# Hybrid encoder layer: ScalarE copies PV's results at the end of their own quarter, and makes V in the second quarter

## The chip, the cores and the metric

One NeuronCore of a Trainium2 chip runs the whole layer in one launch. The metric is device time in microseconds (us) from launch to end, the median of several executions. A profile of one further execution gives the span from the first to the last instruction and what each engine did in it.

## The reference, cut to what matters

```python
# per layer: half FFN, mixer (convolution group + attention), half FFN, final norm
h = h + 0.5 * g1 * _swiglu(_modulate(h, sh1, s1), ffn1_wg, ffn1_wu, ffn1_wd)
z = _modulate(h, shm, smx) @ w_in                 # -> u | cq | ckv | kr
a = u[..., :C_CONV] * sigmoid(u[..., C_CONV:])
a = depthwise_conv(a, conv_w, width 31) + conv_b  # 512 channels
a = silu(_layernorm(a, g_conv_ln, b_conv_ln))
q, k, v = up-projections of cq and ckv, q and k RMS-normed by head, rotary on 32 of 96
def one_block(qblk):
    s = einsum('bqhd,bkhd->bhqk', qblk, k) * scale
    p = softmax(s, axis=-1)
    return einsum('bhqk,bkhd->bqhd', p, v)
h = h + gm * (concatenate([a, att], axis=-1) @ w_out)
h = h + 0.5 * g2 * _swiglu(_modulate(h, sh2, s2), ffn2_wg, ffn2_wu, ffn2_wd)
```

Sequence 1024, model width 1024, 8 heads with 96-wide q and k and 64-wide v.

## The kernel before

**Stages.** The two feed-forward halves take most of the time. Between them stands the mixer; its attention part runs from about 884 us to 1176 us of the span, and the change lies there alone. Every engine has an order of its own, written out by hand, and the engines meet through semaphores.

**Turns and quarters.** `run_units` gives each engine four turns `i` of two heads each. Turn 0 and turn 3 (the last) are written out, and turns 1 and 2 are a loop with a register. A turn has four quarters `m`: quarter `m` handles head `m // 2` of the turn and the half `m % 2` of the 1024 queries. So quarters 0 and 2 are called even, and quarters 1 and 3 odd. A quarter has four steps `p`. Over them:

- PE turns the next head's q and k in even quarters (`pe_turn_head`, L1710, one unit in each step), makes the products for the next quarter's maxima (`pe_max`, L1594), this quarter's scores (`pe_scores`, L1635, six matmuls), and PV of the quarter before (`pe_pv`, L1657, four matmuls) into bank 6. In step 3 it also turns the row of maxima (`pe_max_row`, L1616), between the two halves of that step's PV.
- ScalarE (ACT) casts each turned head unit (`act_head_unit`, L1721), writes the row of maxima into the augmented queries (`act_max`, L1623), takes the exponentials (`act_exp`, L1644), copies PV's finished bank to `grow` (`act_pv_copy`, L1666), spreads V to `vs` (`act_v`, L1688), and makes the products of convolution taps for channel chunks 2 and 3 (`act_prod`, L1806): 2, 1, 2 and 1 in the steps of an even quarter, 0, 1, 2 and 1 in those of an odd one.
- VectorE (DVE) reduces the maxima (`dve_max`, L1602), makes the low part of head units (`dve_head_unit`, L1728, even quarters) or a convolution tap of chunks 0 and 1 (`dve_tap`, L1826, one in each step of an odd quarter), three parts of the reciprocal of PV's denominators in steps 0 to 2 (`dve_pv_recip`, L1673), and in step 3 the scaling into `att` (`dve_pv_scale`, L1681). All of it is for the PV result of the quarter before.
- GpSimd (POOL) adds the products to `cv` (`pool_conv`, L1815 and L1816, two instructions for each product) and, at the start of odd quarters, makes the slots of a coming head (`pool_slots`, L1760, L1762, L1766).

**What ties them.** The waits that the change touches:

```python
def act_pv_copy(e, i, m):
    e.wait_ge(pv_mm, i * 4 + m)                # the PV of quarter m is finished
    if not (isinstance(i, int) and i == 0 and m == 1):
        e.wait_ge(pv_out, i * 4 + (m - 1))     # VectorE has scaled the result before it
```

`pe_pv` may begin a quarter's PV only when the copy of the result before it is made (`pv_copied`) and the exponentials of that quarter are all there. `pe_turn_head` number n waits until VectorE has made the low part of head unit n - 1 (`qk_lo`), which waits for the cast on ScalarE. `act_prod` number n waits until POOL has added product n - 2 (`conv_add`), and `pool_conv` waits for its product (`prod_ok`). `pe_max` waits for the reduction before it (`s_max`), `act_v` for the last PV that reads the old V (`pv_mm`), and the first PV with a new V for `v_ok`.

Before the change ScalarE copies the result of quarter `m - 1` in step 0 of quarter `m`, so behind the product of step 3, and makes V in step 3 of an odd quarter, between `act_max` and the last exponential.

Of the kernel before, what the change touches and what calls it, by code (L numbers as in the profile page):

```python
# [39 lines left out]
def build(nc, A, out):  # L40
# [5 lines left out]
    NH = S // HALF  # L46
# [31 lines left out]
    with ExitStack() as ctx:  # L78
# [1492 lines left out]
        TURNS = NHD // 2  # L1571
        AUG = QK + 1

        def at(i, m):

            return (i + m // NU, m % NU)
# [42 lines left out]
        def act_max(e, i, m):  # L1619
            i, m = at(i, m)  # L1620
            hp, h = divmod(m, NH)
            e.wait_ge(m_row, i * 4 + (m + 1))
            e.activation(qkT[QK:AUG, hp, 0, HI, h * HALF:(h + 1) * HALF], ps[0:1, MISC], ACT.Copy).then_inc(m_ok, 1)  # L1623
# [15 lines left out]
        def act_exp(e, i, m, p):  # L1639
            e.wait_ge(s_mm, i * 16 + (m * 4 + p + 1))  # L1640
            if p == 0 and not (isinstance(i, int) and i == 0 and m < 2):
                e.wait_ge(pv_mm, i * 4 + (m - 1))
            b = 2 + 2 * (p % 2)
            e.activation(EX[m % 2][:, 2 * p:2 * p + 2], ps[:, b:b + 2], ACT.Exp).then_inc(s_exp, 1)  # L1644
# [16 lines left out]
        def act_pv_copy(e, i, m):  # L1661

            e.wait_ge(pv_mm, i * 4 + m)
            if not (isinstance(i, int) and i == 0 and m == 1):
                e.wait_ge(pv_out, i * 4 + (m - 1))
            e.activation(grow[:, 0:HALF], ps[:, 6], ACT.Copy).then_inc(pv_copied, 1)  # L1666
# [16 lines left out]
        def act_v(e, i, hp, first=False):  # L1683

            hd = i * 2 + hp
            if not first:
                e.wait_ge(pv_mm, hd * 2 - 2)
            e.activation(vs[:, hp, :, 0:VH], vn[:, :, bass.ds(hd, 1), :].rearrange("p t a d -> p t (a d)"), ACT.Copy)\  # L1688
                .then_inc(v_ok, 1)
# [27 lines left out]
        def act_head_unit(e, i, hp, n, first=False):  # L1717
            u, bank = head_unit(n, first)
            hp_, m, tok = head_place(hp, u)
            e.wait_ge(qk_turned, i * 8 + (hp * 4 + n + 1))  # L1720
            e.activation(qkT[0:QK, hp_, m, HI, tok], ps[0:QK, bank], ACT.Copy, scale=gains[0:QK, m:m + 1])\  # L1721
                .then_inc(qk_hi, 1)
# [74 lines left out]
        def products(m, p0, p1):  # L1797

            start = m // NH * TT + m % NH * sum(PRODUCTS[0])
            return range(start + sum(PRODUCTS[m % NH][:p0]), start + sum(PRODUCTS[m % NH][:p1]))  # L1800

        def act_prod(e, i, n, first):
            c, k = 2 + n % 2, 1 + n // 2
            if not (first and n < 2):
                e.wait_ge(conv_add, i * (2 * TT) + (n - 1))
            e.activation(prod[:, n % 2], ac[:, c, bass.ds(i * TT + k, S)], ACT.Copy,  # L1806
                         scale=cw[:, c, bass.ds(i * TT + k, 1)]).then_inc(prod_ok, 1)
# [60 lines left out]
        def act_ln_square(e, c):  # L1868
            e.wait_ge(ln_mean, 2 * CC)
            e.activation(squares[c], cv[:, c], ACT.Square).then_inc(ln_act, 1)  # L1870
# [29 lines left out]
        def act_ln_swish(e):  # L1900
            for c in range(CC):
                e.wait_ge(ln_dve, 3 + c)
                e.activation(cv[:, c], cv[:, c], ACT.Silu, bias=vect[:, V_LB + c:V_LB + c + 1],
                             scale=vect[:, V_LG + c:V_LG + c + 1]).then_inc(ln_act, 1)
# [9 lines left out]
        def act_wo_hi(e, c):  # L1914
            e.wait_ge(wo_scaled, c + 1)
            if c == 0:
                e.wait_ge(slot_k, NHD + 1)
            if c == 5:
                e.wait_ge(v_ok, NHD)
            if c == 7:  # L1920
                e.wait_ge(pv_mm, 2 * NHD)
            e.activation(wo[:, c, HI], wor[:, c % 2], ACT.Copy).then_inc(wo_hi, 1)
# [5 lines left out]
        def run_units(e, unit):  # L1928

            for m in range(NU):  # L1930
                unit(0, m, True, False)
            with e.Fori(1, TURNS - 1) as i:
                for m in range(NU):
                    unit(i, m, False, False)
            for m in range(NU):
                unit(TURNS - 1, m, False, True)

        def next_head(i, m):

            return (i, 1) if m // NH == 0 else (i + 1, 0)  # L1940
# [178 lines left out]
        def _(e):  # L2119
# [146 lines left out]

            def unit(i, m, first, last):
                for p in range(THALF):
                    if p == 0 and not (first and m < 2):
                        act_pv_copy(e, *at(i, m - 1))  # L2270
                    if m % NH == 0 and not (last and m // NH == 1):
                        act_head_unit(e, *next_head(i, m), p)
                    if p == 3 and not (last and m == NU - 1):
                        act_max(e, i, m + 1)
                    if last:
                        for c in WO_HI_AT.get((m, p), ())[:1]:
                            act_wo_hi(e, c)
                    if last and m == 2 and p < 2:
                        act_ln_square(e, 2 * p)
                        act_ln_square(e, 2 * p + 1)  # L2280
                    if p == 3 and m % NH == 1 and not (last and m // NH == 1):
                        act_v(e, *next_head(i, m), first=first and m == 1)
                    act_exp(e, i, m, p)
                    if last:
                        for c in WO_HI_AT.get((m, p), ())[1:]:
                            act_wo_hi(e, c)
                    if not last and not (first and m == 0 and p == 0):
                        for n in products(m, p, p + 1):
                            act_prod(e, i, n, first)

            run_units(e, unit)
            act_pv_copy(e, TURNS, -1)
            act_ln_swish(e)
            act_wo_hi(e, KC - 2)
            act_pv_copy(e, TURNS, 0)
# [496 lines left out]
```

## Time and profile before

| what | value |
|---|---|
| median of 3 runs | 1919.88 us (1916.6 to 1920.43) |
| the profiled execution: its own time | 1922.11 us |
| its span, first to last instruction | 1919.9 us |
| mean granted TensorE clock | 0.987 |
| PE busy over the span | 1840.6 us (96%) |
| DVE, ACT, POOL busy over the span | 1392.3, 796.0, 803.7 us |
| stretch 1010 to 1027 us (an odd quarter): PE, DVE, ACT, POOL busy | 15.59, 16.18, 10.62, 16.73 of 17.00 us |
| stretch 1027 to 1044 us (an even quarter): PE, DVE, ACT, POOL busy | 16.45, 14.32, 13.70, 16.29 of 17.00 us |

The shares over the whole span hide that the attention stretch has limits of its own: there PE, DVE and POOL are all busy most of the time, so the rows below are those of single instructions in it. In a timeline row the first number is the start in us from the span's start, the second the duration in us, then engine, line, operation, what it writes and reads, and in brackets the idle time of the engine just before it with what ended it. Durations overlap a little on one engine, because instructions are pipelined.

### The profile page before, as it was taken

How to read it: one execution, taken by the hardware profiler on the slowest of the kernel's cores; microseconds unless marked ns; L12 is line 12 of the kernel's file. 1: busy time of each engine (PE TensorE's matmuls, PEld its weight loads, DVE VectorE, ACT ScalarE, POOL GpSimd, SP SyncE). 2: the span in 40 equal slices, each digit the busy share in tenths (PEclk: the TensorE clock that was granted, in tenths of full speed). 3: DMA queues.
4: the chain of work that ended last, by engine and by line, in shares of the span. 5: the costliest groups of instructions: out<-in, count | busy, mean ns of one | idle time of the engine just before them, and what ended most of it. 6: DMA issues, size and time to landing. Idle time of an engine off the chain costs nothing.

```text
span 1919.9 us, 22681 instructions
## 1 busy us (share of the span) xinstructions
PE 1840.6 (96%) x8043; PEld 1471.2 (77%) x8043; DVE 1392.3 (73%) x1774; ACT 796.0 (41%) x1248; POOL 803.7 (42%) x605
## 2 busy tenths in 40 slices
PE   4999999999999999997999999999999999999997
PEld 3788888878888878985665566877888888888886
DVE  5678888876777785776888877358656555577778
ACT  4542232223344554246676643154332323334453
POOL 1076655666200010019999941014566556520000
PEclk9999999999999999997999999999999999999999
DMA  9045666545653442000000023112333323476333
GB/s 351 12 143 184 222 210 206 198 154 199 251 209 94 124 171 69 4 1 0 1 1 0 0 68 152 66 55 85 107 110 110 107 85 110 170 249 228 96 108 125
DMA packets 132795, 232.11 MB, mean 121 GB/s; under 512 B 8780, under 2 KB 66227, under 8 KB 132434
## 3 DMA queue, kind: packets, MB, share of 16 engines
q1 hardware_dynamic: 132500, 230.73, 35.5%
q8 instruction: 62, 1.02, 0.2%
q14 instruction: 43, 0.35, 0.1%
q10 hardware_dynamic: 190, 0.01, 0.0%
HBM read 177.75 MB, written 52.95 MB: 120 GB/s over the span
## 4 chain that ended last, share of the span: by engine, by line
PE 43%; DVE 6%; POOL 2%; issue 2%; ACT 2%; DMA 0%; DVEq 0%; ACTq 0%; POOLq 0%
PE ps L502 20%; PE ps L854 9%; PE ps L2752 4%; PE ps L1657 3%; PE ps L376 2%; PE ps L1635 2%; DVE cv L1826 1%; PE ps L1594 1%; DVE grow L1673 1%; DVE att L1681 1%; POOL rqk L1751 0%; DVE negmax L1602 0%; ACT prod L1806 0%; PE ps L1710 0%; DVE H L2598 0%
## 5 line engine op out<-in xcount | busy, mean ns | idle before, releaser
L502 PE MATMUL ps<-T,ring 128*128 128x512 f32 x1920 | 441.8, 389 | 0.0
L502 PEld LDWEIGHTS ps<-T,ring 128*128 128x128 f32 x1920 | 360.3, 188 | 75.0 <-DVE ring L479 0.2
L502 PE MATMUL ps<-B,ring 128*128 128x512 f32 x1440 | 338.1, 391 | 5.7 <-DVE SG L561 4.4
L502 PEld LDWEIGHTS ps<-B,ring 128*128 128x128 f32 x1440 | 269.4, 188 | 65.1 <-issue 9.5
L954 POOL TENSOR_SCALAR stat<-stat 128x1 f32<-128x1 f32 x32 | 10.7, 333 | 550.8 <-ACT XS L879 260.0
L568 POOL TENSOR_TENSOR HID<-HID,SG 128x512 f32<-128x512 f32 x80 | 122.2, 1527 | 262.4 <-DVE HID L553 151.5
L854 PE MATMUL ps<-PW 128*128 128x512 f32 x924 | 217.3, 389 | 0.0
L854 PE MATMUL ps<-PT 128*128 128x512 f32 x900 | 212.0, 390 | 0.0
L854 PEld LDWEIGHTS ps<-PW 128*128 128x128 f32 x924 | 173.3, 188 | 36.0
L479 DVE TENSOR_TENSOR ring<-sums,ring 128x512 fp32r<-128x512 f32 x160 | 162.9, 1027 | 52.0 <-ACT ring L473 52.0
L854 PEld LDWEIGHTS ps<-PT 128*128 128x128 f32 x900 | 168.5, 188 | 34.8
L473 ACT ACTIVATE ring<-sums 128x512 fp32r<-128x512 f32 x160 | 97.0, 627 | 158.8 <-PE ps L502 139.8
L522 ACT ACTIVATE SG<-SG 128x512 f32<-128x512 f32 x80 | 50.6, 633 | 245.7 <-DVE SG L553 98.5
L1657 PE MATMUL ps<-E,vs 128*128 128x512 f32 x256 | 125.7, 607 | 10.4 <-ACT grow L1666 10.4
L1602 DVE TENSOR_REDUCE negmax<-ps 128x1 f32<-128x1024 f32 x64 | 77.3, 1211 | 37.5 <-PE ps L1594 37.4
L479 DVE TENSOR_TENSOR ring<-rawu,ring 128x512 fp32r<-128x512 f32 x60 | 66.6, 1120 | 51.9 <-ACT ring L473 51.9
L1635 PE MATMUL ps<-qkT 97*128 97x512 f32 x384 | 103.5, 406 | 0.0
L701 ACT ACTIVATE PW<-adat 128x512 fp32r<-128x512 f32 x77 | 48.6, 631 | 123.9 <-PE ps L854 91.7
L1815 POOL TENSOR_TENSOR cv<-cv,prod 128x512 f32<-128x512 f32 x60 | 88.7, 1478 | 8.8 <-ACT prod L1806 8.6
L701 ACT ACTIVATE PT<-adat 128x512 fp32r<-128x512 f32 x75 | 47.4, 631 | 107.2 <-PE ps L854 92.1
L2752 PE MATMUL ps<-wo,mixT 128*128 128x512 f32 x384 | 88.0, 390 | 2.7 <-DVE mixT L2562 2.7
L708 DVE TENSOR_TENSOR PT<-adat,PT 128x512 fp32r<-128x512 f32 x84 | 58.7, 708 | 43.0 <-ACT PT L701 43.0
(337 smaller groups left out, 3303.0 us busy)
## 6 DMA issues: line engine op xcount, KB each, us to landing
adat<-ffn_hidden SPq DMA_DIRECT2D x154, 256.0 KB, 2.7
ada_raw<-in_w_ada SPq DMA_DIRECT2D x56, 512.0 KB, 4.0
rawg<-in_ffn_wg SPq DMA_DIRECT2D x22, 1024.0 KB, 5.5
rawu<-in_ffn_wu SPq DMA_DIRECT2D x22, 1024.0 KB, 5.3
ffn_hidden<-HID SPq DMA_DIRECT2D x84, 256.0 KB, 2.7
ffn_hidden<-base SPq DMA_DIRECT2D x66, 256.0 KB, 2.6
H<-in_x SPq DMA_DIRECT2D x16, 512.0 KB, 6.8
h_saved_rows<-H SPq DMA_DIRECT2D x16, 512.0 KB, 2.6
```

The costliest lines, as they stand in the source:

```text
L473: e.activation(ring[:, n % RING, HI], src, ACT.Copy).then_inc(f.w_hi.sem, 1)
L479: e.tensor_tensor(ring[:, n % RING, LO], src, ring[:, n % RING, HI].bitcast(F32), ALU.subtract).then_inc(f.w_lo.sem, 1)
L502: mm = e.matmul(ps[:, product_bank(M, k)], ring[:, place % RING, wx, kc], RIGHT[k][:, xx, kc], start=(kc == 0 and i == 0), stop=(kc == HC ...
L568: e.tensor_tensor(HID[:, q], HID[:, q], SG[:, q], ALU.mult).then_inc(f.w_mul.sem, 1)
L701: e.activation(pair(f, n)[:, 0, HI], left_raw(n), ACT.Copy).then_inc(f.cut_hi.sem, 1)
L708: e.tensor_tensor(pair(f, n)[:, side, LO], raw, pair(f, n)[:, side, HI].bitcast(F32), ALU.subtract)\
L854: mm = e.matmul(bank_of(j, t), pair(f, n)[:, 0, ax, t * P:(t + 1) * P], pair(f, n)[:, 1, wx], start=(g == 0 and i == 0), stop=(g == GROUPS ...
L1602: e.tensor_reduce(negmax[:, m % 2, p:p + 1], ps[:, b:b + NH].rearrange("p b k -> p (b k)"), AX_X, ALU.max, negate=True).then_inc(s_max, 1)
L1635: mm = e.matmul(ps[:, 2 + 2 * (p % 2) + b], qkT[0:AUG, hp, 1, x, kt * P:(kt + 1) * P], qkT[0:AUG, hp, 0, y, h * HALF:(h + 1) * HALF], star ...
L1657: mm = e.matmul(ps[:, 6], vs[:, hp, kt], EX[(m - 1) % 2][:, kt], start=(kt == 0), stop=(kt == NT - 1))
L1815: e.tensor_tensor(cv[:, c, first_half], cv[:, c, first_half], prod[:, n % 2, first_half], ALU.add)
L2752: mm = e.matmul(ps[:, 4 + m % MB], mixT[:, t % 2, xx, c], wo[:, c, wx, h * HALF:(h + 1) * HALF], start=(c == 0 and k == 0), stop=(c == KC ...
```

## The change

Only ScalarE's order changes. The copy of quarter `m`'s PV result moves from step 0 of the next quarter to step 3 of its own quarter, directly behind the last exponential and ahead of that step's product. V is made in step 1 of an odd quarter instead of step 3. The copy that stood behind the last turn falls away, since the last quarter now makes it itself. The orders of PE, VectorE, POOL and the DMA queues are the same.

```diff
             def unit(i, m, first, last):
                 for p in range(THALF):
-                    if p == 0 and not (first and m < 2):
-                        act_pv_copy(e, *at(i, m - 1))
                     if m % NH == 0 and not (last and m // NH == 1):
                         act_head_unit(e, *next_head(i, m), p)
...
-                    if p == 3 and m % NH == 1 and not (last and m // NH == 1):
+                    if p == 1 and m % NH == 1 and not (last and m // NH == 1):
                         act_v(e, *next_head(i, m), first=first and m == 1)
                     act_exp(e, i, m, p)
+                    if p == 3 and not (first and m == 0):
+                        act_pv_copy(e, i, m)
                     if last:
                         for c in WO_HI_AT.get((m, p), ())[1:]:
                             act_wo_hi(e, c)
...
             run_units(e, unit)
-            act_pv_copy(e, TURNS, -1)
             act_ln_swish(e)
             act_wo_hi(e, KC - 2)
             act_pv_copy(e, TURNS, 0)
```

## Rows read from the trace of the kernel before

**Rows 1.** Waits of PE and ACT, 884 to 1177 us: total us, times, longest.
```profile
PE ps L1657 <- ACT grow L1666: 10.4, 13, 1.1
...
ACT grow L1666 <- DVE att L1681: 3.0, 6, 1.2
```

**Rows 2.** Timeline of PE in the first turn and around two copies in the loop.
```profile
927.13 1.95 PE L1657 MATMUL ps<-E,vs 128*128 128x512 f32 x4 [0.62 <-ACT grow L1666]
...
1008.65 1.54 PE L1635 MATMUL ps<-qkT 97*128 97x512 f32 x6
1010.82 1.96 PE L1657 MATMUL ps<-E,vs 128*128 128x512 f32 x4 [0.63 <-ACT grow L1666]
...
1027.07 1.98 PE L1657 MATMUL ps<-E,vs 128*128 128x512 f32 x4 [0.85 <-ACT grow L1666]
1028.89 0.60 PE L1710 MATMUL ps<-ident,slot 128*96 128x128 f32 x4
...
1029.80 1.54 PE L1635 MATMUL ps<-qkT 97*128 97x512 f32 x6
1031.18 1.88 PE L1657 MATMUL ps<-E,vs 128*128 128x512 f32 x4
```

**Rows 3.** Timeline of ACT around the same two copies.
```profile
1009.05 1.14 ACT L1806 ACTIVATE prod<-ac,cw 128x1024 f32 x1
1010.10 0.58 ACT L1666 ACTIVATE grow<-ps 128x512 f32<-128x512 f32 x1
...
1014.66 1.02 ACT L1644 ACTIVATE E<-ps 128x1024 f32<-128x1024 f32 x1 [3.07 <-PE ps L1635]
...
1023.70 0.63 ACT L1688 ACTIVATE vs<-vn 128x512 f32 x1
1024.24 1.01 ACT L1644 ACTIVATE E<-ps 128x1024 f32<-128x1024 f32 x1
1025.15 1.15 ACT L1806 ACTIVATE prod<-ac,cw 128x1024 f32 x1
1026.42 0.60 ACT L1666 ACTIVATE grow<-ps 128x512 f32<-128x512 f32 x1
1026.91 0.68 ACT L1721 ACTIVATE qkT<-ps,gains 96x512 fp32r<-96x512 f32 x1
```

**Rows 4.** Timeline of DVE in the odd quarter between them.
```profile
1011.30 1.35 DVE L1673 RECIPROCAL grow<-grow 64x192 f32<-64x192 f32 x1
1013.28 1.23 DVE L1602 TENSOR_REDUCE negmax<-ps 128x1 f32<-128x1024 f32 x1 [0.63 <-PE ps L1594]
1014.53 1.79 DVE L1826 SCALAR_TENSOR_TENSOR cv<-ac,cw,cv 128x1024 f32<-128x1024 f32 x1
...
1018.61 1.37 DVE L1826 SCALAR_TENSOR_TENSOR cv<-ac,cw,cv 128x1024 f32<-128x1024 f32 x1
...
1022.27 2.41 DVE L1826 SCALAR_TENSOR_TENSOR cv<-ac,cw,cv 128x1024 f32<-128x1024 f32 x1
1024.61 1.78 DVE L1681 TENSOR_TENSOR att<-grow 64x512 f32 x1
...
1027.62 0.75 DVE L1728 SCALAR_TENSOR_TENSOR qkT<-ps,gains,qkT 96x512 fp32r<-96x512 f32 x1
```

**Rows 5.** Timeline of POOL, loop, and one wait of the last turn.
```profile
1010.27 2.12 POOL L1815 TENSOR_TENSOR cv<-cv,prod 128x512 f32<-128x512 f32 x1 [0.52 <-ACT prod L1806]
...
1013.60 1.05 POOL L1760 TENSOR_TENSOR slot<-kn,rqk 128x512 f32 x1
...
1017.63 1.27 POOL L1815 TENSOR_TENSOR cv<-cv,prod 128x512 f32<-128x512 f32 x1
...
1027.47 1.27 POOL L1815 TENSOR_TENSOR cv<-cv,prod 128x512 f32<-128x512 f32 x1
...
1043.61 2.12 POOL L1815 TENSOR_TENSOR cv<-cv,prod 128x512 f32<-128x512 f32 x1 [0.63 <-ACT prod L1806]
...
1133.36 2.39 POOL L1850 TENSOR_TENSOR prod<-prod 128x1024 f32<-128x1024 f32 x1 [0.40 <-ACT pp L1870]
```

## Prediction

> **What bounds the kernel now.** I read the waits first, then the timelines of the four engines over two quarters of the loop. The waits say what is there to be won: PE waits for ScalarE's copy 13 times, 10.4 us together, and no other wait on it in the stretch is as large. The copy itself waits for VectorE's scaling 6 times [rows 1]. So two kinds of crossing between quarters have to be told apart.
>
> From an even quarter to an odd one (5 crossings with a product in front of the copy), the copy starts at 1010.10, when the product begun at 1009.05 is through [rows 3]. PE starts PV at 1010.82. Where it need not wait, PV starts 1.38 behind the first of the scores (1029.80 to 1031.18), so here it could have started at 1008.65 + 1.38 = 1010.03 [rows 2]. That is 0.79 lost, and the four matmuls take 0.08 longer behind a stall (1.96 against 1.88): 0.87 in all.
>
> From an odd quarter to an even one in the loop, the product is through at 1025.15 + 1.15 = 1026.30, but VectorE's scaling ends at 1024.61 + 1.78 = 1026.39, and the copy starts at 1026.42 [rows 3, 4]. The last release is the scaling's. The product in front of it costs next to nothing there: 0.1 at most.
>
> Why is the scaling so late? VectorE has no idle time from the reduction at 1013.28 on, and POOL is as full: between its additions at 1010.27 and 1043.61, 33.34 us apart and one turn of two quarters, it stands idle for 0.63 only [rows 4, 5]. And the two hinder each other. A tap (L1826) takes 1.79, 1.37 and 2.41 in one quarter, and POOL's addition 2.12 instead of 1.27 [rows 4, 5]; the end of each such tap lies about 1.1 behind the end of a POOL instruction. The tap at 1018.61 shows it best: POOL's addition runs from 1017.63 to 1018.90, and the tap ends at 1019.98. So I take it that they exclude each other, and that a tap's end is set by POOL's schedule.
>
> The Trainium skill says the same (SBUF — State Buffer, "Who interferes with whom"): a VectorE instruction with two SBUF inputs and a GpSimd instruction that reads SBUF lock each other out, and whichever starts first holds the port to its end. The trace agrees, with 1.37 and 2.41 for the same tap. By that rule alone an earlier VectorE only waits longer for POOL; were the port shared by bandwidth, the 0.87 above would carry on to the scaling.
>
> **The change part by part.**
>
> 1. Copy ahead of the product, even to odd. The product no longer stands in front. The copy starts when the exponential is through, about when the product started (1009.05), and ends near 1009.65, before PE wants bank 6 at 1010.03. PE gains 0.87 at that place. What does it make of it? The reduction at 1013.28 waited for PE; it now starts when the reciprocal of 1011.30 + 1.35 is nearly through, about 1012.57, or 0.71 earlier. Its tap asks for the port at 1013.82, after POOL's slot instruction has begun (1013.60, 1.05 long), gets it at 1014.65, and is through at 1015.75 instead of 1014.53 + 1.79 = 1016.32. The next tap asks 0.57 earlier, at 1018.04 instead of 1018.61. But POOL began its addition at 1017.63 and holds on to 1018.86, as before. The tap ends at 1019.98, as before, and so do the two instructions after it, the tap of 1022.27 and the scaling [rows 4, 5]. I take 0 of the 0.87 for the end; the bounds are 0 and 0.87 in each of 5 crossings. The product, now 0.47 later (1010.10 to the next start), makes POOL's addition ready 0.5 later than 1010.27. It had to wait until the tap on VectorE was through anyhow (2.12 long instead of 1.27, so 0.85 of cover), and I take nothing for that either; without this cover it is 0.47 each.
>
> 2. Copy ahead of the product, odd to even. V is gone from this place, so the exponential starts 0.54 earlier (1023.70 against 1024.24). But the copy still has to wait for the scaling, at 1026.39, and starts at 1026.42. ScalarE runs its queue in order: behind the waiting copy now stand the product, the first head unit, the next quarter's first exponential and its two products. The product that used to fill the time from 1025.15 starts at 1026.92 instead, and the head unit at 1027.97 instead of 1026.91, so 1.06 later. VectorE's part of it (1027.62) starts at 1028.67 and ends at 1029.42, and PE's next turn (1028.89), which waits for it, starts 0.14 later (the distance from the copy's end at 1010.68 to PE at 1010.82), at 1029.56: 0.67 late [rows 2 to 4]. Taking the shorter release (0.05, from 1027.02 to 1027.07) it is 0.58; I use 0.65. The cushion that hides the rest is the 0.4 between the old end of VectorE's part, 1028.37, plus the release, and 1028.89. If all of the 1.06 counted it would be that; if PE had other slack it would be 0. PE is back to back through the even quarter, so what is lost at its beginning stays lost. POOL's addition of that product moves from 1027.47 to 1028.1, also 0.65 late [rows 5], so the two stay in step. There are five crossings of this kind (after quarters 1 and 3 of turns 1 and 2, and after quarter 3 of turn 0): 5 x 0.65 = +3.25.
>
> 3. The crossing after quarter 1 of turn 0 has no scaling before it. There PE waits in front of 927.13 by as much as in the even ones [rows 2], V's removal brings the exponential 0.54 forward, and nothing holds the copy. PE gains 0.87, in an even quarter, where PE itself sets the pace: -0.87.
>
> 4. V in step 1. ScalarE stood idle for 3.07 before that exponential [rows 3], and V takes 0.63; cost 0. If that cover were gone it would be 0.54 in each odd quarter, the same as before.
>
> 5. The last turn has no products, so the copies stand where they did. Only V matters, after its quarter 1. ScalarE's squares come 0.54 earlier, and POOL, which waits 0.40 for them at 1133.36 [rows 5], can use just 0.40. The chain that ended last goes on from there to the output projection without a gap: -0.40.
>
> Sum: -0.87 + 3.25 + 5 x 0 - 0.40 = +1.98, say +2.0 us. The profiled execution, 1922.11 us with 2.2 around its span, would come to 1924.1. That execution is 2.2 above the median of the runs, so against the median the forecast is 1919.88 + 2.0 = 1921.9 us. A tenth of a per cent: no more than 0.2% (3.84 us) can be told from no change here, and I forecast "same".
>
> **The rivals.**
>
> Gain kept: VectorE's earlier start reaches the scaling, because a tap gets the port one POOL instruction sooner. It decides at the tap of 1014.53: were its request 0.22 earlier than my 1013.82, it would get in ahead of the slot instruction of 1013.60. Then 5 x 0.87 comes back: -0.87 - 4.35 + 3.25 - 0.40 = -2.4, or 1917.5 us. The floor is POOL's own work: with its idle time (0.52 to 0.63 a turn) gone in five places, about -2.9, and nothing lost from odd to even, it is -0.87 - 2.9 - 0.40 = -4.2, or 1915.7. For it: POOL's idle time shows that the pace isn't yet POOL's. Against it: the 0.4 between 1017.63 and my 1018.04.
>
> Held by cover: the late head unit costs PE nothing, because PE or VectorE makes the delay good before the end of the even quarter. Then -0.87 - 0.40 = -1.3, or 1918.6 us. Against it: PE's rows follow each other without a gap in even quarters.
>
> Slower: POOL is the pacer, and lateness of a product is not hidden at even ends. Then each turn of two quarters takes 0.65 + 0.47 more, 5 x 1.12 = 5.6, less the 0.87 and 0.40 of parts 3 and 5, so +4.3, or 1924.2 us. It decides at POOL's addition at 1010.27: if it is no longer held up by the tap, or if POOL isn't drained when the tap of step 0 asks for the port, VectorE's whole quarter moves. Its cushion is the 0.52 to 0.63 that POOL stands idle there [rows 5], which speaks against it.
>
> **How the numbers follow.** Forecast 0.50, gain kept 0.17, held by cover 0.17, slower 0.16. The range takes in all but the floor of the one and what lies beyond the other: 1916.6 to 1924.4 us. The forecast alone spans 1921.5 to 1923.9: that is 0.58 and 1.06 in place of 0.65, five times each. Faster by over 0.2% needs nearly the whole floor: 0.07. Slower by over 0.2% is the slower case and a little of the forecast's edge: 0.16. Within 0.2%: 0.77.
>
> **What the profile after would show.** PE's waits for the copy fall from 13 to about 7 (those of the first turn and of five even quarters gone): those of odd to even stay at 0.85 to 1.0. The copy's waits for the scaling (3.0 us) grow by over 1 us in each of five crossings, since the product no longer fills them. PE shows a new wait of about 0.5 in front of L1710 for L1728, five times. The taps of steps 2 and 3 keep their places relative to POOL, 1.1 behind the end of its addition. The distance from one PV behind an odd quarter to the next (33.3 now) becomes 34.0. V at step 1 adds no time in front of an exponential.
>
> The prediction is wrong if that distance stays or shrinks, if the scaling comes earlier relative to the last exponential of the even quarter before it, or if the new wait in front of L1710 is missing.

## The result and the profile after

| | before | after |
|---|---|---|
| median of 9 runs each | 1920.01 us (1916.6 to 1922.33) | 1924.74 us (1923.46 to 1927.36) |
| profiled execution: time, span | 1922.11, 1919.9 us | 1924.38, 1922.2 us |

The ratio is 1.0027, 95% interval 1.0018 to 1.0037: 4.7 us or a quarter of a per cent slower, clear of no change. The forecast was 1921.9 us and "same"; its range ended at 1924.4.

The waits of PE, ACT and POOL over 884 to 1182 us, after (total us, times, longest):

```profile
ACT prod L1806 <- POOL cv L1816: 14.2, 15, 2.2
ACT grow L1666 <- DVE att L1681: 13.3, 9, 1.8
...
PE ps L1657 <- ACT grow L1666: 6.7, 8, 1.1
...
PE ps L1710 <- DVE qkT L1728: 4.5, 7, 1.8
...
POOL wor L1912 <- DMA wor<-in_w_out: 30.4, 5, 19.1
POOL cv L1815 <- ACT prod L1806: 14.0, 13, 2.4
```

and the last of these in before, over 884 to 1177 us:

```profile
POOL cv L1815 <- ACT prod L1806: 8.6, 12, 1.7
```

PE's wait for the copy fell from 10.4 to 6.7 us, the copy's own wait for the scaling rose from 3.0 to 13.3 [rows 1], and POOL's wait for products from 8.6 to 14.0. Four timelines show the odd quarter of [rows 2 to 5] again, 0.57 us earlier here. ACT, after:

```profile
974.29 0.60 ACT L1666 ACTIVATE grow<-ps 128x512 f32<-128x512 f32 x1 [0.54 <-DVE att L1681]
...
1008.49 0.59 ACT L1666 ACTIVATE grow<-ps 128x512 f32<-128x512 f32 x1
1008.96 1.15 ACT L1806 ACTIVATE prod<-ac,cw 128x1024 f32 x1
...
1022.52 0.58 ACT L1623 ACTIVATE qkT<-ps 1x512 fp32r<-1x512 f32 x1 [0.62 <-PE ps L1616]
...
1025.91 0.60 ACT L1666 ACTIVATE grow<-ps 128x512 f32<-128x512 f32 x1 [1.76 <-DVE att L1681]
1026.41 1.15 ACT L1806 ACTIVATE prod<-ac,cw 128x1024 f32 x1
1027.47 0.67 ACT L1721 ACTIVATE qkT<-ps,gains 96x512 fp32r<-96x512 f32 x1
...
1037.89 1.15 ACT L1806 ACTIVATE prod<-ac,cw 128x1024 f32 x1 [0.32 <-POOL cv L1816]
...
1041.13 0.58 ACT L1623 ACTIVATE qkT<-ps 1x512 fp32r<-1x512 f32 x1 [1.52 <-PE ps L1616]
...
1056.62 0.58 ACT L1623 ACTIVATE qkT<-ps 1x512 fp32r<-1x512 f32 x1 [0.54 <-PE ps L1616]
```

PE, after:

```profile
1009.48 1.88 PE L1657 MATMUL ps<-E,vs 128*128 128x512 f32 x4
...
1026.56 1.98 PE L1657 MATMUL ps<-E,vs 128*128 128x512 f32 x4 [0.92 <-ACT grow L1666]
1028.97 0.64 PE L1710 MATMUL ps<-ident,slot 128*96 128x128 f32 x4 [0.43 <-DVE qkT L1728]
...
1040.45 0.65 PE L1616 MATMUL ps<-ident,negmax 128*128 128x128 f32 x4
```

DVE, after:

```profile
971.40 2.79 DVE L1681 TENSOR_TENSOR att<-grow 64x512 f32 x1
...
1013.19 2.00 DVE L1826 SCALAR_TENSOR_TENSOR cv<-ac,cw,cv 128x1024 f32<-128x1024 f32 x1
...
1017.48 1.96 DVE L1826 SCALAR_TENSOR_TENSOR cv<-ac,cw,cv 128x1024 f32<-128x1024 f32 x1
...
1024.04 1.78 DVE L1681 TENSOR_TENSOR att<-grow 64x512 f32 x1
...
1039.64 0.75 DVE L1728 SCALAR_TENSOR_TENSOR qkT<-ps,gains,qkT 96x512 fp32r<-96x512 f32 x1 [0.29 <-ACT qkT L1721]
```

POOL, after:

```profile
971.13 1.27 POOL L1815 TENSOR_TENSOR cv<-cv,prod 128x512 f32<-128x512 f32 x1
972.35 1.29 POOL L1816 TENSOR_TENSOR cv<-cv,prod 128x512 f32<-128x512 f32 x1
976.00 1.79 POOL L1815 TENSOR_TENSOR cv<-cv,prod 128x512 f32<-128x512 f32 x1 [2.36 <-ACT prod L1806]
...
1010.19 1.65 POOL L1815 TENSOR_TENSOR cv<-cv,prod 128x512 f32<-128x512 f32 x1 [1.19 <-ACT prod L1806]
...
1017.10 1.27 POOL L1815 TENSOR_TENSOR cv<-cv,prod 128x512 f32<-128x512 f32 x1
...
1027.64 1.26 POOL L1815 TENSOR_TENSOR cv<-cv,prod 128x512 f32<-128x512 f32 x1 [0.70 <-ACT prod L1806]
1028.87 1.28 POOL L1816 TENSOR_TENSOR cv<-cv,prod 128x512 f32<-128x512 f32 x1
1030.24 1.29 POOL L1815 TENSOR_TENSOR cv<-cv,prod 128x512 f32<-128x512 f32 x1
...
1133.55 2.39 POOL L1912 TENSOR_TENSOR wor<-wor,gm_row 128x1024 f32<-128x1024 f32 x1 [19.11 <-DMA wor<-in_w_out]
```

From even to odd (1008.49) the copy stands in front of the product and PE starts PV at 1009.48 with no wait. From odd to even (1025.91) the copy waits 1.76 for the scaling, the product and the head unit wait behind it, POOL stands idle for 0.70 and PE waits 0.43 in front of L1710.

**Where the time went.** The row of maxima (ACT L1623, step 3 of each quarter) marks the quarters, so I measured from one to the next. The even quarter above took 1041.13 - 1022.52 = 18.61 us, the odd one behind it 1056.62 - 1041.13 = 15.49. Sums over the attention part, in us, each worked out from the starts of L1623 ("first": the one around the crossing after quarter 1 of turn 0; "even": the five behind an odd quarter; "odd": the six odd ones; "last": from the last but one row of maxima to the 25th matmul of PE's output projection):

| kernel | first | even | odd | last |
|---|---|---|---|---|
| before | 17.53 | 88.90 | 94.32 | 52.13 |
| after | 16.66 | 92.90 | 94.81 | 53.28 |
| after, second execution (below) | 16.65 | 92.90 | 95.64 | 52.52 |

After against before that is -0.87 + 4.00 + 0.49 + 1.15 = +4.77, and -0.88 + 4.00 + 1.32 + 0.39 = +4.83 in the second execution: both lie near the 4.7 between the medians. That the terms other than the 4.00 add up so well twice is partly chance, as shown at parts 1 and 5 below.

The first two quarters are left out of the table. They took 35.3 us in before, 34.2 and 35.1 in the two executions after, and 32.6 in four kernels below; with them the attention part is 3.6 and 4.6 us longer than in before. What differs there is the execution, not the kernel: up to the row of maxima that ends these quarters, e2 and e3 below have every engine's order as in before, and yet took 32.6. The clock that TensorE was granted differs with it. The same window of before, then of e3 (us, PE, PEld, DVE, ACT and POOL busy, then the granted clock, DMA share and GB/s):

```profile
905.00:912.00 7.00, 6.37 (x15) 4.25 (x16) 2.90 (x3) 3.67 (x4) 5.34 (x5) 0.52 0.00 0
```

```profile
905.00:912.00 7.00, 4.31 (x19) 2.59 (x17) 3.37 (x4) 5.22 (x6) 5.83 (x6) 1.00 0.00 0
```

### The profile page after: what moved, and what is told of

It reads as the page before. It is cut to its first block, busy times and chain, and to the rows that moved or that the text cites. A ratio compares the mean times of both kernels' runs of the same rounds, so it can differ in the third digit from the quotient of the medians.

```text
span 1922.2 us, 22679 instructions
## 1 busy us (share of the span) xinstructions
PE 1839.5 (96%) x8043; PEld 1468.1 (76%) x8043; DVE 1398.6 (73%) x1774; ACT 796.1 (41%) x1248; POOL 799.9 (42%) x605
## 4 chain that ended last, share of the span: by engine, by line
PE 36%; DVE 6%; POOL 6%; issue 5%; DMA 1%; ACT 1%; POOLq 0%; ACTq 0%; DVEq 0%
PE ps L502 19%; PE ps L854 9%; PE ps L2751 4%; POOL cv L1816 3%; PE ps L376 1%; PE ps L1657 1%; POOL cv L1815 1%; PE ps L1635 1%; DVE grow L1673 1%; DVE T L935 1%; POOL slot L1766 0%; POOL rqk L1751 0%; DMA wor<-in_w_out 0%; DVE wo L1926 0%; DVE cv L1826 0%
```

## The experiments

"Median" is that of all timed runs of that kernel; "before" is the kernel before in the same job. Even, odd and last are the sums of the table above.

**V alone, even copies alone, odd copies alone, both without the odd.** The diff splits into three. `e1_v_only` is before with V in step 1. `e2_even_only` is before with this, and `e3_odd_only` has the same two lines with `== 1`, and no copy behind the last turn:

```diff
-                    if p == 0 and not (first and m < 2):
+                    if p == 0 and m % NH == 0 and not (first and m < 2):
                         act_pv_copy(e, *at(i, m - 1))
...
                     act_exp(e, i, m, p)
+                    if p == 3 and m % NH == 0 and not (first and m == 0):
+                        act_pv_copy(e, i, m)
```

`e9_even_and_v` is e2 with V in step 1.

> V is made in step 1 of odd quarters, and the copies stay in step 0 of the next quarter. Theory A (the loss comes from the copy that waits for the scaling at the end of odd quarters, with the product and the head unit queued behind it): no loss, 0 to -0.5 us against the kernel before, the gain being in the last turn alone. Rival C (V's move costs, by what it does to the last turn, where the profile after is 1.15 us later than at that turn's first quarters): +1 to +1.5 us.

> Only the copies of even quarters move to the end of their own quarter, ahead of the product; those of odd quarters and V stay. Theory A: PE's five stalls of 0.6 us behind even quarters vanish, and the time stays within 0.7 us of the kernel before, because the scaling at the end of the next odd quarter comes no earlier relative to the even quarter's last exponential. Rival B (it is the even quarters' product, 0.47 us later, that costs POOL's time): +0.7 to +2.4 us.

> Only the copies of odd quarters move to the end of their own quarter; those of even quarters and V stay. Theory A: the head unit comes 1.06 us later in five crossings, PE loses 0.65 to 0.85 us in each, and the first crossing gives back 0.87, so +2.4 to +3.4 us. Rival B (the loss is in the even quarters): less than +1 us.

> The harmless half of the change: the copies of even quarters move to the end of their own quarter and V moves, the copies of odd quarters stay in step 0 of the next. Theory A: even quarters take 17.8 us and odd ones 15.5 in the loop, as in the kernel before, and the time stays within 1 us of it. If the two halves of the change only cost together, the even quarters take 18.6.

| kernel | median, before in the job | ratio, 95% | first | even | odd | last |
|---|---|---|---|---|---|---|
| e1_v_only | 1919.62, 1921.22 | 0.9994, 0.9981 to 1.0007 | 17.61 | 88.99 | 95.00 | 51.89 |
| e2_even_only | 1921.63, 1921.22 | 1.0007, 0.9995 to 1.0019 | 17.64 | 89.10 | 94.76 | 52.27 |
| e3_odd_only | 1922.98, 1921.22 | 1.0012, 1.0002 to 1.0022 | 17.64 | 92.83 | 94.97 | 52.27 |
| e9_even_and_v | 1921.01, 1920.37 | 1.0005, 0.9992 to 1.0018 | 17.64 | 89.08 | 94.75 | 53.17 |

The odd copies alone carry the whole loss in the even quarters: 92.83 against 88.90. The same crossing in e3 shows the same wait on PE as after:

```profile
1029.15 1.98 PE L1657 MATMUL ps<-E,vs 128*128 128x512 f32 x4 [0.90 <-ACT grow L1666]
1031.56 0.64 PE L1710 MATMUL ps<-ident,slot 128*96 128x128 f32 x4 [0.43 <-DVE qkT L1728]
```

The even copies bring nothing that lasts, although they take away their stalls. V alone changes no quarter of the loop. The first crossing shows its gain of 0.87 in no kernel that has only the odd copies or only V (e1, e3, e9); but these three are also three of the four with the fast beginning, so that both are needed isn't shown.

All four have one odd quarter in turn 0 of 16.2 us (15.58 in before), which is what lifts their odd sums, and all four have short first quarters (32.6 us). In front of that odd quarter stands a scaling that took 3.04 us, and that also in e1 and e3, where the even copies stand in their old place. With the short first quarters e3's attention part is 2.1 us longer than that of before, and without them 4.8; its median is 1.8 us longer, with an interval from 0.4 to 4.2. The short beginning belongs to the executions that were traced, as said above; why that scaling takes 3.04 us in all four stays open.

**The change again.** `e5_after_again` is the kernel after, unchanged, for a second trace.

> The changed kernel once more, for its trace. Two things in the first trace of it were in no theory: one odd quarter that began 0.7 us late behind a scaling of 2.79 us, and a load of 512 KB of the output weights that took 4.9 us instead of 3.6 in the last turn. If they belong to the change they come again at the same places; if they are chance they don't. The quarters of the loop should repeat to 0.1 us: 18.6 us for an even one, 15.5 for an odd one.

One execution, 1926.89 us. The even quarters repeat to 0.01 or better (18.68, 18.56, 18.62, 18.59, 18.45), so 18.6 is no accident. The odd ones don't: 15.49, 16.29, 15.56, 16.30, 15.56, where the first trace had one of 16.27. In front of each of the long ones stands a scaling that took 2.8 instead of 1.5 to 1.7 us, as at 971.40 above.

**Taking the port contention away.** In `e6_small_adds_before` and `e7_small_adds_after` POOL adds 8 columns of each half, not all 512, so most of this part of the convolution is left out:

```diff
-            first_half, second_half = slice(0, HALF), slice(HALF, S)
+            first_half, second_half = slice(0, 8), slice(HALF, HALF + 8)
```

> The kernel before with POOL's additions of the convolution products cut to 8 of 512 columns each, so that this part of the convolution is left out and POOL holds nothing up. Theory A (POOL's additions and VectorE's taps exclude each other, and this makes the scaling late): the taps take 1.28 us each and the scaling 0.7, and two quarters still take about 33.3 us, since the copy then waits for the product in both kinds of crossing. Rival D (the scaling is late by VectorE's own work): taps and scaling keep their 1.4 to 2.4 us.

> The changed kernel with the same small additions. Theory A: without POOL in the way, the copy follows the exponential in both kinds of crossing, PE has no stall for it and two quarters take about 31.5 us, 1.8 less than the kernel before has with small additions, so the change would win 9 to 10 us over the stretch. Rival D: two quarters take 34.0 to 34.2 us, as with full additions.

One execution each: 1916.77 and 1906.83 us. The same edit that costs 4.7 us gains 9.9 between these two. DVE of e6, where [rows 4] had 1.37, 2.41 and 1.78:

```profile
1014.02 1.28 DVE L1826 SCALAR_TENSOR_TENSOR cv<-ac,cw,cv 128x1024 f32<-128x1024 f32 x1
...
1017.60 1.28 DVE L1826 SCALAR_TENSOR_TENSOR cv<-ac,cw,cv 128x1024 f32<-128x1024 f32 x1
1018.80 0.68 DVE L1681 TENSOR_TENSOR att<-grow 64x512 f32 x1
```

And a window of four quarters of e7 (us, PE busy, PEld, DVE, ACT and POOL busy, then the granted clock, DMA share and GB/s):

```profile
942.00:1009.00 67.00, 67.00 (x258) 43.41 (x257) 57.33 (x52) 48.63 (x56) 16.26 (x50) 1.00 0.00 1
```

Without POOL in its way VectorE is early, the scaling is through before the copy wants it, and PE is busy for 67.00 of 67.00 us: a pair of quarters takes 31.24 (16.53 + 14.71) against 33.0 in e6 (17.45 + 15.57). So what makes the change a loss is the tie with POOL. The cut takes away two things at once, though: POOL's hold on the port, and POOL's pace (it is busy for 16.26 of 67.00 us here). This pair doesn't tell them apart.

**The scaling ahead of the last tap.** `e4_scale_first` is after with the scaling made before the tap of step 3 in an odd quarter; `e11_before_scale_first` is the same on before.

```diff
                     elif not last:
+                        if p == 3 and not (first and m < 2):
+                            dve_pv_scale(e, *at(i, m - 1))
                         dve_tap(e, i * DTT + (DT + m // NH * 2 + p // 2), (p % 2,))
...
                         if p == 3:
-                            dve_pv_scale(e, *at(i, m - 1))
+                            if m % NH == 0 or last:
+                                dve_pv_scale(e, *at(i, m - 1))
```

> The changed kernel, with VectorE's scaling ahead of the tap in step 3 of odd quarters. Theory A: the scaling is through 1.5 to 2 us earlier, the copy follows the exponential at once in both kinds of crossing, nothing waits behind it, and PE's stalls go; POOL's idle time (0.5 to 0.6 a turn of two quarters) bounds the gain: -3 to -5 us against the kernel before. Rival B (the late products are the cost, not the wait for the scaling): no faster than the kernel before.

> The kernel before with the scaling of odd quarters ahead of the tap in step 3, and nothing of the change. It tells what the scaling's place is worth without the moved copies. Theory A: the copy then waits for the product instead (0.1 us earlier than for the scaling), PE's stalls stay, and two quarters take 33.2 to 33.4 us, the time within 1 us of the kernel before.

| kernel | median, before in the job | ratio, 95% | first | even | odd | last |
|---|---|---|---|---|---|---|
| e4_scale_first | 1920.3, 1921.22 | 1.0001, 0.999 to 1.0012 | 16.66 | 88.83 | 94.01 | 52.93 |
| e11_before_scale_first | 1921.89, 1920.37 | 1.001, 0.9997 to 1.0022 | 17.53 | 89.38 | 94.31 | 53.03 |

The copy of e4 no longer waits at the odd ends of the loop, and the +4.00 of the even quarters is gone: so it came from the wait for the scaling. The gain of 3 to 5 us that I expected isn't there either. Only the quarter without products shows the gain, with 16.98 (17.83 in before); the four in the loop took 17.86 to 18.10 (17.76 to 17.78). On before the same order brings nothing. ACT of e4 shows why the gain of the loop doesn't stay:

```profile
1022.32 0.59 ACT L1666 ACTIVATE grow<-ps 128x512 f32<-128x512 f32 x1
...
1028.16 1.15 ACT L1806 ACTIVATE prod<-ac,cw 128x1024 f32 x1 [1.28 <-POOL cv L1816]
```

The copy is early, and 6 us later a product waits 1.28 for POOL with the next head unit queued behind it: POOL, whose instructions follow each other without a gap from 1023.00 on, is the pacer of that quarter, as I read it.

**Which of the two that are late costs the time?** `e12_product_behind_head` is after with the product of step 3 of an odd quarter made behind the first head unit, instead of ahead of it:

```diff
                         act_head_unit(e, *next_head(i, m), p)
+                        if p == 0 and not (first and m == 0):
+                            j, mj = at(i, m - 1)
+                            for n in products(mj, 3, 4):
+                                act_prod(e, j, n, first)
...
-                    if not last and not (first and m == 0 and p == 0):
+                    if not last and not (first and m == 0 and p == 0) and not (p == 3 and m % NH == 1):
```

> The changed kernel, with the product of step 3 in odd quarters moved behind the first head unit of the next quarter, so that behind the waiting copy stands the head unit and then the product. It parts the two ways in which the copy's wait can cost 0.8 us a crossing. If it costs by the late head unit alone, PE's wait in front of L1710 and the loss go, and even quarters of the loop take 17.8 us again. If it costs by the late product (POOL adds it later, and ScalarE's second product of the next quarter, which stands ahead of the next head unit, waits for that addition), the head unit of step 1 comes even later, and even quarters take 18.8 to 19.0 us instead of 18.6.

Median 1926.67 us against 1921.81, ratio 1.003 (1.0018 to 1.0042). ACT of e12, behind the same copy:

```profile
1026.38 0.60 ACT L1666 ACTIVATE grow<-ps 128x512 f32<-128x512 f32 x1 [1.76 <-DVE att L1681]
1026.88 0.67 ACT L1721 ACTIVATE qkT<-ps,gains 96x512 fp32r<-96x512 f32 x1
1027.45 1.14 ACT L1806 ACTIVATE prod<-ac,cw 128x1024 f32 x1
```

PE and POOL of e12:

```profile
1028.85 0.60 PE L1710 MATMUL ps<-ident,slot 128*96 128x128 f32 x4
...
1033.92 0.64 PE L1710 MATMUL ps<-ident,slot 128*96 128x128 f32 x4 [0.90 <-DVE qkT L1728]
```

```profile
1028.66 1.28 POOL L1815 TENSOR_TENSOR cv<-cv,prod 128x512 f32<-128x512 f32 x1 [1.25 <-ACT prod L1806]
```

PE's first wait is gone, POOL's idle time grew from 0.70 to 1.25, and the four even quarters of the loop took 19.09, 19.10, 19.02 and 19.10 instead of 18.6. The fifth even quarter, in the last turn, has no products of its own: there the head unit alone counts, and it went from 18.45 back to 17.84 (before: 17.83). So the two paths come apart: in the loop a quarter gets longer by what POOL stands idle (0.70, and 0.13 for the next product, for +0.8; 1.25 for +1.3), and without products by PE's lateness, 0.62.

**Two attempts to use it.** `e8_early_product` is e4 with the product of step 3 in an even quarter made ahead of the row of maxima. `e10_scale_in_step2` is e8 with the scaling of even quarters made in step 2.

```diff
+                    early = p == 3 and m % NH == 0 and not last
+                    if early:
+                        for n in products(m, p, p + 1):
+                            act_prod(e, i, n, first)
                     if p == 3 and not (last and m == NU - 1):
                         act_max(e, i, m + 1)
...
-                    if not last and not (first and m == 0 and p == 0):
+                    if not last and not early and not (first and m == 0 and p == 0):
```

```diff
                         if p == 3:
-                            if m % NH == 0 or last:
+                            if last:
                                 dve_pv_scale(e, *at(i, m - 1))
...
                             dve_pv_recip(e, *at(i, m - 1), p)
+                            if p == 2 and m % NH == 0 and not last:
+                                dve_pv_scale(e, *at(i, m - 1))
```

> The kernel with the scaling ahead of the tap, and in even quarters the product of step 3 ahead of the row of maxima, where ScalarE stood idle for 1.5 us. Theory A with POOL as the pacer of what is left: POOL's idle time of 1.2 us at the end of even quarters goes, but the first tap then waits for POOL, so two quarters take 32.7 to 33.2 us instead of 33.3, and the time is 1 to 3 us below the kernel before. If POOL isn't the pacer, nothing changes against the kernel with the scaling first (two quarters 33.4 us).

> The kernel with the early product, whose scaling once took 8.5 us at the end of an even quarter while POOL's additions followed each other without a gap, and whose loop otherwise took 32.7 us for two quarters. Here the scaling of even quarters stands directly behind the third reciprocal in step 2, 4 us ahead of the copy that needs it. Theory A: a scaling that loses the port several times in a row no longer reaches the copy, no quarter stands out, two quarters take 32.7 us, and the time is 3 to 5 us below the kernel before. If the 8.5 us came from something else, a quarter of over 20 us comes again.

e8: median 1917.64 us against 1919.87, ratio 0.9992 (0.9977 to 1.0007), not to be told from before. In its trace the odd quarters of the loop fell to 14.54 and the even ones stood at 17.3 to 18.4 (32.7 to 33.0 for an odd one and the even one behind it, 33.3 in before), but one odd quarter took 22.80. The traced execution took 1924.47 us, the longest of the twelve (1911.26 to 1924.47), so that quarter need not be in all of them. I expected 1 to 3 us less than before; that is neither shown nor excluded. e10: 1933.48 against 1920.37, ratio 1.0064 (1.0049 to 1.0079), with odd quarters of 18.4 to 19.1, where I expected 3 to 5 us less. Both show the same thing, below.

## Why the prediction was wrong

The two kinds of crossing, and the copy that waits with a queue behind it, were right. Three terms of the sum were not: part 2, which priced a late odd copy by PE's path (0.65) and took POOL to stay in step, where POOL's path ends last (0.8 to 0.9); part 1, taken as 0; and part 5, with the sign wrong in the first trace. Of the 2.8 us missing they make 0.75, 0.49 and 1.55 in the first trace, 0.75, 1.32 and 0.79 in the second. By the parts:

1. **Even to odd, taken as 0 in five crossings.** Right for its reason. PE's stall of 0.87 is gone (PV at 1009.48 without a wait), VectorE's tap of step 1 took 2.00 instead of 1.79, and the tap at 1017.48 again ended 1.07 behind POOL's addition (1019.44 and 1018.37), as forecast. The cover for the late product held too: POOL stood idle for 1.19 instead of 0.52 in front of its addition, but that took 1.65 instead of 2.12 and ended at 1011.84, which is 0.55 ahead of 1010.27 + 2.12 = 1012.39 in before, like the rest of the quarter (0.57). The odd quarters of the loop take 15.49 or 15.56 in e2, against 15.57. The rule of the Trainium skill that was named (SBUF — State Buffer, "Who interferes with whom") agrees: with POOL nearly off the port, in e6, the same taps take 1.28. What I missed is the even end itself. There the scaling (1.68 long at that place before) sometimes misses the port once more, at 971.40 with 2.79, and ends behind the last exponential. The copy waits 0.54 for it, the product behind the copy is late, POOL stands idle for 2.36 (976.00) instead of the 0.52 of [rows 5], and the quarter takes 16.27 to 16.30 instead of 15.57: +0.7, once in one trace and twice in the other, so +0.49 and +1.32 over the six, where the step had 0. e3 has such a scaling (2.80) too, but there the copy stands behind the product, and the quarter stays 15.59. A longer one, 3.04, made a quarter of 16.2 in e1 and e3 as well, with the even copies in their old place. So the moved even copy makes a 2.8 costly, but how often such scalings come, in either kernel, isn't shown by one or two traces.

2. **Odd to even, 5 x 0.65 = +3.25.** It measured +4.00. The step itself is exact: PE's next turn of a head came 2.41 behind PV's start (1026.56 to 1028.97) instead of 1.82 [rows 2], and PV itself 0.06 later behind the row of maxima (4.04, with 3.98 before): 0.65 together. What failed is the sentence that POOL's addition moves by the same 0.65, "so the two stay in step". Measured from the row of maxima POOL's addition came 0.74 later (1027.64 - 1022.52 = 5.12, with 1027.47 - 1023.09 = 4.38 in before), and the next product came 0.13 too late for the one after (1030.24, where 1028.87 + 1.28 less the usual overlap of 0.04 is 1030.11). The row in before:

```profile
1023.09 0.58 ACT L1623 ACTIVATE qkT<-ps 1x512 fp32r<-1x512 f32 x1 [0.65 <-PE ps L1616]
```

   From there POOL has no gap to make it good. What the prediction overlooked is a wait of `pe_max_row`: in an even quarter it waits for the low part of the last head unit, which stands on ScalarE behind a product that waits for POOL. After the change that product waits 0.32 for POOL (1037.89), the low part ends at 1039.64 + 0.75 = 1040.39, and PE turns the row of maxima at 1040.45. So in the four quarters of the loop POOL's path ends last, with 0.79 to 0.92 each; only in the fifth, without products, does PE's own path show, with 0.62. That is my 0.65.

3. **First crossing, -0.87.** Measured 17.53 to 16.66, the number forecast, and 16.65 and 16.66 again in e5 and e4. In e12, e8 and e10, which have both moves and something more, it is 17.08 to 17.38, so the number isn't as firm as it looks.

4. **V in step 1, 0.** Right: e1 leaves the loop's quarters as they were. V at 1010.90 fills a wait for PE's scores.

5. **Last turn, -0.40.** It measured +1.15 and +0.39. V's gain is there, up to the next row of maxima (16.00 to 15.57 and 15.48), but the chain that ended last has another link after:

```profile
1128.62 4.86 DMA wor<-in_w_out
```

I took ScalarE's squares as POOL's last release. After the change it is a load of 512 KB, on which POOL waits 19.11 us. In before, e1, e2, e3, e5, e10 and e11 that load took 3.45 to 3.6 us, in after, e4, e8, e9 and e12 it took 4.65 to 5.00. V earlier brings a second load of 512 KB closer behind it (2.34 instead of 2.86 us), and every long one is in a kernel with V moved. But e1, e5 and e10 have V moved as well and a short one. So that the earlier V causes the long load is suggested, not shown.

   What the load costs is plain from where PE's output projection begins, behind the last but one row of maxima: 45.6 to 45.8 us in kernels without V moved (45.69 in before), 45.3 to 45.5 with V moved and a short load, 46.5 to 46.8 with V moved and a long one. In e5, with the short load, it is 45.29: the forecast 0.40 less, to the digit. That its stretch is still 0.39 longer has another reason. From the first to the 24th matmul there PE took 7.0 us instead of 5.3, and the granted clock was at half for 3.4 us of it. PE had been idle for 1.95 us in front of the first. A window of e5, in the columns of the windows above, the clock being 0.70:

```profile
1174.00:1178.00 4.00, 3.40 (x10) 2.71 (x11) 3.97 (x5) 0.99 (x2) 0.00 (x0) 0.70 0.33 135
```

   In before and after PE had been idle for the same 1.95 us, and the clock was 1.00 in these matmuls; e11, without V moved, has the dip too (0.79 in 1170 to 1174 and in 1174 to 1178), and its stretch took 53.03 us, where before took 52.13. So the first trace's +1.15 is the long load less V's gain, and the second's +0.39 is my -0.40 and 0.79 more that goes with the clock, which no run ties to the change.

The sum by the measured terms is -0.87 + 4.00 + (0.49 or 1.32) + (1.15 or 0.39) = +4.8, where the forecast had +1.98. Only the first two terms are the same in both traces.

**The rivals.** Gain kept: false; e2 has the even copies alone, and its odd quarters gain 0.09 at most. Held by cover: false, the even quarters got 4.00 longer; neither POOL nor PE has cover there. Slower, at 1924.2 us, came nearest in number, in part by luck, and its first half is what happened: POOL's schedule sets the pace, so a late product isn't hidden. Its place was wrong, and its 0.47 for each even end didn't come. It was to decide at POOL's addition at 1010.27; there POOL's idle time did grow from 0.52 to 1.19 (1010.19), and the quarter was no longer for it. The loss came at the addition at 1027.47, at the other end, where POOL had been without a gap.

**The signs named beforehand.** PE's waits for the copy fell from 13 to 8 (7 forecast). The copy's waits at the odd ends are 1.76 to 1.84. The wait in front of L1710 is there, with 0.43. A pair of quarters takes 34.1 (18.62 + 15.49) where 33.3 was and 34.0 was forecast.

No kernel tried that computes the whole layer is shown faster than before. A scaling that is early and leaves POOL its pace was not found.

## What to carry to other kernels

A wait placed early in an in-order queue delays everything that used to stand ahead of it: before moving an instruction up, look whether its own release comes in time, and if not, what it will hold up. When one wait makes two engines late, follow both to the end of the stage and charge the longer path; here PE's path, with its visible wait of 0.43, was the shorter, and the idle time of POOL, which had none there before, gave the loss to within 0.1. And a cover that is measured in one quarter (the 0.52 of POOL at the even end) has to be looked up at the other kind of quarter as well.

## What the runs showed of the hardware

A VectorE instruction can lose the port that it shares with POOL several times in a row. In e8 one scaling, 0.68 alone, took 8.53 us. DVE, and then ACT of e8:

```profile
937.86 8.53 DVE L1681 TENSOR_TENSOR att<-grow 64x512 f32<-64x512 f32 x1
```

```profile
946.49 0.60 ACT L1666 ACTIVATE grow<-ps 128x512 f32<-128x512 f32 x1 [5.76 <-DVE att L1681]
```

POOL of e8, the first and the last of seven instructions that follow each other without a gap:

```profile
937.84 1.27 POOL L1815 TENSOR_TENSOR cv<-cv,prod 128x512 f32<-128x512 f32 x1
...
944.36 1.49 POOL L1766 TENSOR_TENSOR slot<-qn,rqk 128x768 f32<-128x768 f32 x1
```

POOL's seventh instruction ended at 945.85 and the scaling 0.54 later, and the copy waited 5.76 for it: this is the quarter of 22.80. PE stood idle for 5.81 us meanwhile, and from 944.6 on its granted clock was at half for 6.8 us, so the quarter lost more than the wait. In e10 the first tap of an odd quarter did the same:

```profile
1016.55 6.14 DVE L1826 SCALAR_TENSOR_TENSOR cv<-ac,cw,cv 128x1024 f32<-128x1024 f32 x1
```

POOL ran there back to back from 1016.04 to 1021.61. In before the same taps get in after one POOL instruction, so POOL without a gap isn't enough for it; what decides who wins at the boundary between two POOL instructions stays open. It may be that POOL's half microsecond of idle time in a pair of quarters, which looked like slack, was also a moment at which VectorE could get in; no run tests that.
